# The pooling's per-head map and scale folded once into the output weight's last 256 rows

## The chip, the cores and the metric

The kernel runs on one core of a Trainium2 chip, in float32 from end to end. The metric is the device time of one execution in microseconds, the median of the runs; less is better. TensorE is called PE in the profile's rows (PEld is its weight load), VectorE is DVE, ScalarE is ACT, GpSimd is POOL and SyncE, which issues most DMAs, is SP.

## The reference, cut to what matters

One layer of a hybrid decoder trunk on 2048 tokens of width 1024. A normalised input is projected by one matrix into the columns of three head groups (windowed attention, retention, causal pooling), their outputs are concatenated and go through an output matrix, and a feed-forward block and a final normalisation follow. The change touches the pooling group alone:

```python
# u: (tokens, 256), four groups of 64 columns with windows 2, 4, 8, 16
groups.append(win_sum / cnt - uf[..., sl])
pooled = jnp.stack(groups, axis=2)
mixed = jnp.einsum('bsgc,gcd->bsgd', pooled, pool_w)        # a 64x64 map per group
mixed = mixed.reshape(B, S, POOL_WIDTH) * pool_scale        # a factor per column
...
y = jnp.concatenate([ya, yr, yp], axis=-1)                  # yp is `mixed`
return x + y @ w_out
```

The last 256 rows of `w_out` are multiplied by `mixed` and by nothing else, and nothing nonlinear lies between `pooled` and that product. So `(pooled @ W_g * scale) @ w_out_rows` equals `pooled @ (W_g @ diag(scale) @ w_out_rows)`.

## The kernel before, in words

Every large product is made of three products of rounded parts (high x low, low x high, high x high; lines 2145 to 2147 in the helper `three`), so every weight block and every activation exists as a `_hi` and a `_lo` tile. ACT makes the `_hi` (`split_hi`, line 958, for weights), DVE the `_lo` as source minus `_hi` (`split_lo`, line 1670).

The mixer runs over four quarters of 512 tokens (`q`); then come the feed-forward's up products and down products, more than half of the time. Each engine has one program, written out by hand in the order in which it is to run; engines meet by semaphores alone. `Events.now(q, i)` is the count after event `i` of quarter `q`.

Weights come in 27 units of 128x1024 per quarter. SP loads unit `u` into one of three `stage` slots (`load_weights`, line 559) once the split of unit `u-3` is over, ACT and DVE split it into a ring of six slots. Units 0 to 5 and 18 feed the products `proj_T` (outputs transposed: three q blocks, k, v, and the two pooling blocks), 6 to 17 feed `proj_G`, 19 to 26 are the rows of `w_out`: 25 and 26 are the pooling's.

In the first quarter everything starts at once: SP issues the inputs, tables, constants, the four 64x64 maps (`poolw`, line 577), the table of positional bias rows to DRAM and back (`store_rows` line 581, `load_bias` line 587, which waits for the store to have landed), and the units, all on one queue. Of the eight PSUM banks, three (`dense`) take the large products; S0, S1 hold scores, T0, T1 transposes, OB outputs.

The program of TensorE in a quarter begins with four `proj_T`, then `row_factors` (line 2166: the row factors spread over a bank), `proj_T(4)`, the first attention scores (`att_scores(q, 0)`, line 2242, into S0 and S1), `proj_T(5)`, the next scores. Retention and output products come last, and among them `pool_mix` (line 2346): one 128x512 float32 product per pooling half and quarter, block-diagonal `poolw` with the `pooled` tile, into T1. ACT then writes `T1 * pscale` as the high part (`yP_high`, line 1080), DVE the low part (`yP_low`, line 1606), into `hT_hi` and `hT_lo`, which the output products 8 to 15 read. `pooled` is the tile `vT`, used again for both halves and for v in the next quarter.

Of the kernel before, what the change touches and what calls it, by code (L numbers as in the profile page):

```python
# [7 lines left out]
P = 128  # L8
D = 1024
SEQ = 2048  # L10
HEAD = 64
NQH, NKV, NRET = 6, 2, 6
# [98 lines left out]
def build(nc, x, xt, wmix, wup, wdn, cst, tab, onehot, gmix, gmlp, gfin, sinks, rel_bias, pool_w, pool_scale, out):  # L111
    x2_dram = nc.dram_tensor("x2_dram", (SEQ, D), F32).ap()
    u_dram = nc.dram_tensor("u_dram", (NPASS, NK, NPAIR // GP, P, GP, HALF), F32).ap()
    rows_dram = nc.dram_tensor("bias_rows_dram", (NQH, P * 384), F32).ap()

    with ExitStack() as ctx:
# [47 lines left out]
        pt = work("pt", 76928, [P, 2, 2 * 3 * P])  # L164
        vT = work("vT", 83072, [P, QT])
# [90 lines left out]
        s_pm = sem("s_pm")  # L256

# [28 lines left out]
        comb_done = Events(sem("comb_done"), 8)  # L286
        max_done = Events(sem("max_done"), 8)
# [3 lines left out]
        den_done = Events(sem("den_done"), 8)  # L291
        rinv_done = Events(sem("rinv_done"), 8)
# [27 lines left out]
        ya_done = Events(sem("ya_done"), 4)  # L320
        y_done = Events(sem("y_done"), 4)
# [7 lines left out]
        mix_done = Events(sem("mix_done"), 2)  # L329
# [203 lines left out]
        def _(sp):  # L533
# [258 lines left out]
        def _(pool):  # L792
# [56 lines left out]
            def kz_of(q, b):  # L849

                pool.wait_ge(qk_done.sem, qk_done.now(q, b))
                pool.wait_ge(ru_done.sem, ru_done.before(q, b))
# [92 lines left out]
        def _(act):  # L945
# [53 lines left out]
            def evac_T(q, t):  # L999
# [4 lines left out]
                else:  # L1004
                    act.wait_ge(mix_done.sem, mix_done.before(q, 1))
# [173 lines left out]
            def mixer_act(q, last):  # L1179
# [7 lines left out]
                split_hi(q, 4)  # L1187
                evac_T(q, 2)
# [4 lines left out]
                split_hi(q, 8)  # L1193
                evac_T(q, 4)
# [231 lines left out]
        def _(dve):  # L1426
            for e in (wlo_done, carried, s_evac, xlo_done, x2_evac, sc_done, comb_done, max_done, pt_evac, nmax_done, sde_done, den_done, rinv_done, pn_done,
# [1238 lines left out]
```

## Time and profile before

| What | Value |
|---|---|
| Median of 3 runs | 2020.3 us (2020.28 to 2021.57) |
| Span of the profiled execution | 2018.4 us |
| Median less span (what lies around the span) | 1.9 us |
| TensorE busy | 2006.9 us, 99% |
| DVE / ACT / POOL busy | 70% / 44% / 9% |
| The chain that ended last | 98% TensorE |
| Granted TensorE clock | 0.999 mean |

The profile gives one execution. Its span goes from the first instruction to the last; the device time of the runs is a little longer. "Busy" of TensorE counts a matmul from start to its modelled end, and matmuls overlap, so the distance from one start to the next is what a matmul costs the engine, not its listed duration.

### The profile page before, as it was taken

How to read it: one execution, taken by the hardware profiler on the slowest of the kernel's cores; microseconds unless marked ns; L12 is line 12 of the kernel's file. 1: busy time of each engine (PE TensorE's matmuls, PEld its weight loads, DVE VectorE, ACT ScalarE, POOL GpSimd, SP SyncE). 2: the span in 40 equal slices, each digit the busy share in tenths (PEclk: the TensorE clock that was granted, in tenths of full speed). 3: DMA queues.
4: the chain of work that ended last, by engine and by line, in shares of the span. 5: the costliest groups of instructions: out<-in, count | busy, mean ns of one | idle time of the engine just before them, and what ended most of it. 6: DMA issues, size and time to landing. Idle time of an engine off the chain costs nothing.

```text
span 2018.4 us, 26877 instructions
## 1 busy us (share of the span) xinstructions
PE 2006.9 (99%) x9964; PEld 1691.7 (84%) x9964; DVE 1416.2 (70%) x2043; ACT 891.2 (44%) x1500; POOL 190.9 (9%) x279
## 2 busy tenths in 40 slices
PE   9999999999999999999999999999999999999998
PEld 8988898889889888888888888888888888888886
DVE  6685578558746977777778677677666668667667
ACT  5433543543354426545456544445333334433333
POOL 2042113203220330000000000000000000000001
PEclk9999999999999999999999999999999999999999
DMA  8133412522252233676856566787957578756572
GB/s 285 56 98 136 142 63 74 193 84 79 100 181 85 93 117 102 149 185 160 181 149 152 136 154 179 178 190 198 396 196 276 197 298 323 287 202 261 200 289 84
DMA packets 101950, 348.64 MB, mean 173 GB/s; under 512 B 10267, under 2 KB 12220, under 8 KB 84412
## 3 DMA queue, kind: packets, MB, share of 16 engines
q1 hardware_dynamic: 99372, 338.27, 52.6%
q10 hardware_dynamic: 2448, 8.65, 1.2%
q8 instruction: 80, 1.31, 0.3%
q14 instruction: 50, 0.41, 0.1%
HBM read 270.21 MB, written 76.68 MB: 172 GB/s over the span
## 4 chain that ended last, share of the span: by engine, by line
PE 98%; DVE 1%; ACT 1%; issue 0%; POOL 0%; POOLq 0%; ACTq 0%
PE bank L2145 30%; PE bank L2147 30%; PE bank L2146 30%; PE bank L2242 1%; PE bank L2270 1%; PE bank L2318 1%; PE bank L2299 1%; PE bank L2321 1%; PE bank L2285 1%; PE bank L2361 1%; PE bank L2326 1%; PE bank L2256 1%; DVE hT_lo L1443 1%; PE bank L2346 0%; PE bank L2135 0%; PE bank L2336 0%
## 5 line engine op out<-in xcount | busy, mean ns | idle before, releaser
L2145 PE MATMUL bank<-h_hi,w_lo 128*128 128x512 f32 x912 | 355.7, 390 | 0.2 <-DVE h_lo L1654 0.2
L2147 PE MATMUL bank<-h_hi,w_hi 128*128 128x512 f32 x912 | 354.9, 389 | 0.0
L2146 PE MATMUL bank<-h_lo,w_hi 128*128 128x512 f32 x912 | 354.9, 389 | 0.0
L2145 PE MATMUL bank<-d_hi,u_lo 128*128 128x512 f32 x896 | 348.5, 389 | 0.0
L2146 PE MATMUL bank<-d_lo,u_hi 128*128 128x512 f32 x896 | 348.5, 389 | 0.0
L2147 PE MATMUL bank<-d_hi,u_hi 128*128 128x512 f32 x896 | 348.5, 389 | 0.0
L1286 ACT ACTIVATE u_hi<-u_raw 128x1024 fp32r<-128x1024 f32 x112 | 118.5, 1058 | 327.7 <-PE bank L2147 315.2
L1906 DVE TENSOR_TENSOR u_lo<-u_raw,u_hi 128x1024 fp32r<-128x1024 f32 x112 | 137.1, 1224 | 179.6 <-ACT u_hi L1286 179.6
L2145 PE MATMUL bank<-ring_hi,hT_lo 128*128 128x384 f32 (+1 forms) x672 | 241.3, 359 | 0.0
L2147 PE MATMUL bank<-ring_hi,hT_hi 128*128 128x384 f32 (+1 forms) x672 | 234.1, 348 | 0.0
L2146 PE MATMUL bank<-ring_lo,hT_hi 128*128 128x384 f32 (+1 forms) x672 | 233.8, 348 | 0.0
L2145 PEld LDWEIGHTS bank<-h_hi,w_lo 128*128 128x128 f32 x912 | 171.2, 188 | 35.8 <-issue 0.4
L2147 PEld LDWEIGHTS bank<-h_hi,w_hi 128*128 128x128 f32 x912 | 171.2, 188 | 35.6
L2146 PEld LDWEIGHTS bank<-h_lo,w_hi 128*128 128x128 f32 x912 | 171.2, 188 | 35.0
L2145 PEld LDWEIGHTS bank<-d_hi,u_lo 128*128 128x128 f32 x896 | 168.2, 188 | 34.9
L2146 PEld LDWEIGHTS bank<-d_lo,u_hi 128*128 128x128 f32 x896 | 168.2, 188 | 34.9
L2147 PEld LDWEIGHTS bank<-d_hi,u_hi 128*128 128x128 f32 x896 | 168.2, 188 | 34.9
L1670 DVE TENSOR_TENSOR ring_lo<-stage,ring_hi 128x1024 fp32r<-128x1024 f32 x108 | 134.0, 1265 | 37.9 <-ACT ring_hi L958 37.4
L1663 DVE TENSOR_TENSOR w_lo<-wraw,w_hi 128x512 fp32r<-128x512 f32 x156 | 104.2, 687 | 76.7 <-ACT w_hi L1105 75.9
L1105 ACT ACTIVATE w_hi<-wraw 128x512 fp32r<-128x512 f32 x156 | 96.7, 626 | 91.7 <-PE bank L2147 87.4
L958 ACT ACTIVATE ring_hi<-stage 128x1024 fp32r<-128x1024 f32 x108 | 109.8, 1053 | 60.2 <-DMA stage<-in_wmix 44.2
L2145 PEld LDWEIGHTS bank<-ring_hi,hT_lo 128*128 128x128 f32 x672 | 126.2, 188 | 11.4 <-issue 2.4
(220 smaller groups left out, 3109.0 us busy)
## 6 DMA issues: line engine op xcount, KB each, us to landing
u_raw<-u_dram SPq DMA_DIRECT2D x56, 1024.0 KB, 4.8
d_raw<-in_wdn SPq DMA_DIRECT2D x56, 1024.0 KB, 6.9
stage<-in_wmix SPq DMA_DIRECT2D x108, 512.0 KB, 4.4
u_dram<-ur SPq DMA_DIRECT2D x32, 1280.0 KB, 9.7
wraw<-in_wup SPq DMA_DIRECT2D x128, 256.0 KB, 3.8
e_raw<-in_wdn SPq DMA_DIRECT2D x24, 1024.0 KB, 8.9
xq<-in_x SPq DMA_DIRECT2D x16, 512.0 KB, 3.6
x_dram<-xq ACTq DMA_DIRECT2D x16, 512.0 KB, 3.0
```

The costliest lines, as they stand in the source:

```text
L958: act.activation(ring_hi[:, SLOT[u % NU], :], stage[:, u % STAGE, :], ACT.Copy).then_inc(whi_done.sem, 1)
L1105: act.activation(w_hi[w_slot(n, k)][:, :, :].rearrange("p c n -> p (c n)"), w_source(n, k), ACT.Copy).then_inc(w_hi_done, 1)
L1286: act.activation(hi[:, cell, :], src[:, 2 * h:2 * h + 2, :], ACT.Copy).then_inc(m_hi_done, 1)
L1443: dve.scalar_tensor_tensor(out=hT_lo[:, c, :], in0=xT[:, c, :], scalar=gcol[:, c:c + 1], in1=hT_hi[:, c, :].bitcast(F32), op0=ALU.mult, op ...
L1663: dve.tensor_tensor(w_lo[s][:, :, :].rearrange("p c n -> p (c n)"), w_source(n, k), w_hi[s][:, :, :].rearrange("p c n -> p (c n)").bitcast ...
L1670: dve.tensor_tensor(ring_lo[:, s, :], stage[:, u % STAGE, :], ring_hi[:, s, :].bitcast(F32), ALU.subtract).then_inc(wlo_done.sem, 1)
L1906: dve.tensor_tensor(lo[:, cell, :], src[:, 2 * h:2 * h + 2, :], hi[:, cell, :].bitcast(F32), ALU.subtract).then_inc(m_lo_done, 1)
L2145: pe.matmul(dst, al, bh, start=(first and k == 0), stop=False, skip_group_check=chain)
L2146: pe.matmul(dst, ah, bl, start=False, stop=False, skip_group_check=chain)
L2147: last = pe.matmul(dst, ah, bh, start=False, stop=(final and k == n - 1), skip_group_check=chain)
L2242: last = pe.matmul((S0, S1)[g][:, P * h:P * h + P], qT[a:a + HEAD, h, b * P:(b + 1) * P], kT[a:a + HEAD, (b + e) * P:(b + e + 1) * P], sta ...
L2256: last = pe.transpose((T0, T1)[k][:, h * P:(h + 1) * P], score_buf(i // 2)[:, k, 256 * h:256 * h + P], ident[:, :])
```

## The change

The map and the scale are multiplied into the last two weight units once, at the beginning of the first quarter. SP loads both units (512 KB each) once more, raw, into a tile `wpool`; ACT multiplies each row by its scale; TensorE multiplies with the transposed maps (four 128x512 float32 products into OB, T0, S0 and S1); ACT copies the four results back into `wpool` and stores them to DRAM as `poolout_dram`. From there SP loads units 25 and 26 in every quarter. `pool_mix` is gone from TensorE's program, and `yP_high` and `yP_low` read `pooled` itself. `wpool` lies where `kz` and a part of `pt` lie, so their first writers wait for the store (`s_poolst`).

```diff
+    poolout_dram = nc.dram_tensor("poolout_dram", (2, P, D), F32).ap()
+        wpool = work("wpool", 70784, [P, 2, D])
             def load_weights(q, u):
                 sp.wait_ge(wlo_done.sem, wlo_done.now(q, u - STAGE))
-                sp.dma_start(stage[:, u % STAGE, :], wmix[u % NU]).then_inc(st_full[u % STAGE].sem, 16)
+                src = wmix[u % NU]
+                if NU - 2 <= u < NU:
+                    sp.wait_ge(s_poolst, 32)
+                    src = poolout_dram[u - (NU - 2)]
+                sp.dma_start(stage[:, u % STAGE, :], src).then_inc(st_full[u % STAGE].sem, 16)
...
-            sp.dma_start(pscale[:, :], pool_scale).then_inc(s_const, 16)
+            sp.dma_start(pscale[:, :], pool_scale).then_inc(s_pool, 16)
             load_weights(0, 4)
             sp.wait_ge(s_pm, 3)
             for g in range(4):
                 a = HEAD * (g % 2)
-                sp.dma_start(poolw[a:a + HEAD, g // 2, a:a + HEAD], pool_w[g]).then_inc(s_const, 16)
+                sp.dma_start(poolw[a:a + HEAD, g // 2, a:a + HEAD], pool_w[g]).then_inc(s_pool, 16)
+            for cc in range(2):
+                sp.dma_start(wpool[:, cc, :], wmix[NU - 2 + cc]).then_inc(s_pool, 16)
...
             def yP_high(q, cc):
-                act.wait_ge(mix_done.sem, mix_done.now(q, cc))
-                act.activation(hT_hi[:, 3 + cc, :], T1[:, :], ACT.Copy, scale=pscale[:, cc:cc + 1]).then_inc(yPhi_done.sem, 1)
+                act.wait_ge(pooled_done.sem, pooled_done.now(q, 2 * cc + 1))
+                act.wait_ge(pool16_done.sem, pool16_done.now(q, 4 * cc + 3))
+                act.wait_ge(tile_done.sem, tile_done.now(q, T_UP1))
+                act.activation(hT_hi[:, 3 + cc, :], pooled[:, :], ACT.Copy).then_inc(yPhi_done.sem, 1)
+
+            def pool_weights_scaled():
+                act.wait_ge(s_pool, 16 * 7)
+                for cc in range(2):
+                    act.activation(wpool[:, cc, :], wpool[:, cc, :], ACT.Copy, scale=pscale[:, cc:cc + 1]).then_inc(s_poolscaled, 1)
+
+            def pool_weights_out():
+                for i in range(4):
+                    cc, half = divmod(i, 2)
+                    act.wait_ge(s_poolmm, i + 1)
+                    act.activation(wpool[:, cc, 512 * half:512 * half + 512], (OB, T0, S0, S1)[i][:, :], ACT.Copy).then_inc(s_poolout, 1)
+                    if half:
+                        act.wait_ge(s_poolout, i + 1)
+                        act.dma_start(poolout_dram[cc], wpool[:, cc, :]).then_inc(s_poolst, 16)
...
                 split_hi(q, 4)
+                if q == 0:
+                    pool_weights_scaled()
                 evac_T(q, 2)
...
                 split_hi(q, 8)
+                if q == 0:
+                    pool_weights_out()
                 evac_T(q, 4)
...
             def yP_low(q, cc):
                 dve.wait_ge(yPhi_done.sem, yPhi_done.now(q, cc))
-                dve.scalar_tensor_tensor(out=hT_lo[:, 3 + cc, :], in0=T1[:, :], scalar=pscale[:, cc:cc + 1],
-                                         in1=hT_hi[:, 3 + cc, :].bitcast(F32), op0=ALU.mult, op1=ALU.subtract).then_inc(yPlo_done.sem, 1)
+                dve.tensor_tensor(hT_lo[:, 3 + cc, :], pooled[:, :], hT_hi[:, 3 + cc, :].bitcast(F32), ALU.subtract).then_inc(yPlo_done.sem, 1)
...
             def att_scores(q, j):
                 if j == 0:
...
                     pe.wait_ge(s_brow, NQH)
+                    pe.wait_ge(s_poolout, 4)
...
-            def pool_mix(q, cc):
...
-                pe.matmul(T1[:, :], poolw[:, cc, :], pooled[:, :], start=True, stop=True).then_inc(mix_done.sem, 1)
+            def pool_weights():
+                pe.wait_ge(s_poolscaled, 2)
+                pe.wait_ge(s_brow, NQH)
+                for i in range(4):
+                    cc, half = divmod(i, 2)
+                    pe.matmul((OB, T0, S0, S1)[i][:, :], poolw[:, cc, :], wpool[:, cc, 512 * half:512 * half + 512],
+                              start=True, stop=True).then_inc(s_poolmm, 1)
...
                 row_factors(q)
+                if q == 0:
+                    pool_weights()
                 proj_T(q, 4)
...
-        "pool_w": a(pool_w)[0], "pool_scale": a(pool_scale).reshape(2, P).T,
+        "pool_w": a(pool_w)[0].transpose(0, 2, 1), "pool_scale": a(pool_scale).reshape(2, P).T,
```

Left out of the diff: waits on `mix_done` become waits on `yPlo_done`, or fall away; `row_factors` and `qk_transposes` no longer wait for `yPlo_done`; seven semaphores of the softmax and of the gate are merged into three with the same instructions; and DVE's `nsink` waits for the five constant loads, no longer for the maps.

TensorE's program in the first quarter, from the last product of `proj_T(3)` on (line 2166 is the row factors, `dg` their diagonal blocks), before:

```order
L2147 MATMUL bank<-hT_hi,ring_hi 128x512
L2166 MATMUL bank<-dg,ones 128x128 [waits s_init,s_brow,diag_done,yPlo_done,qkT_evac]
L2166 MATMUL bank<-dg,ones 128x128 x3
L2145 MATMUL bank<-hT_hi,ring_lo 128x512 [waits z_evac,wlo_done]
...
L2147 MATMUL bank<-hT_hi,ring_hi 128x512
L2242 MATMUL bank<-kT,qT 128x128 [waits R_done,s_brow,pm_done,s_evac,z_evac]
L2242 MATMUL bank<-kT,qT 128x128 x5
```

and after (the lines 2193, 2173 to 2175 and 2270 are the former 2166, 2145 to 2147 and 2242):

```order
L2175 MATMUL bank<-hT_hi,ring_hi 128x512
L2193 MATMUL bank<-dg,ones 128x128 [waits s_init,diag_done,s_brow,qkT_evac]
L2193 MATMUL bank<-dg,ones 128x128 x3
L2372 MATMUL bank<-wpool,poolw 128x512 [waits s_brow,s_poolscaled]
L2372 MATMUL bank<-wpool,poolw 128x512 x3
L2173 MATMUL bank<-hT_hi,ring_lo 128x512 [waits z_evac,wlo_done]
...
L2175 MATMUL bank<-hT_hi,ring_hi 128x512
L2270 MATMUL bank<-kT,qT 128x128 [waits s_poolout,R_done,s_brow,pm_done,s_evac,z_evac]
L2270 MATMUL bank<-kT,qT 128x128 x5
```

Four products stand between the row factors and `proj_T(4)`, and the first scores wait for ACT's four copies (`s_poolout`) as well.

ACT's program at the same time, from the split of unit 4 on, before:

```order
L958 ACTIVATE ring_hi<-stage 128x1024 [waits tile_done,st_full1]
L1007 ACTIVATE qT<-bank 128x512 [waits tile_done]
L958 ACTIVATE ring_hi<-stage 128x1024 [waits tile_done,st_full2]
L997 ACTIVATE rb<-bank 128x512 [waits s_evac,rbmm_done]
L958 ACTIVATE ring_hi<-stage 128x1024 [waits wlo_done,tile_done,st_full0]
L958 ACTIVATE ring_hi<-stage 128x1024 [waits wlo_done,tile_done,st_full1]
L958 ACTIVATE ring_hi<-stage 128x1024 [waits wlo_done,tile_done,st_full2]
L1007 ACTIVATE vT<-bank 128x512 [waits mix_done,tile_done]
```

and after:

```order
L968 ACTIVATE ring_hi<-stage 128x1024 [waits tile_done,st_full1]
L1098 ACTIVATE wpool<-wpool,pscale 128x1024 [waits s_pool]
L1098 ACTIVATE wpool<-wpool,pscale 128x1024
L1017 ACTIVATE qT<-bank 128x512 [waits tile_done]
L968 ACTIVATE ring_hi<-stage 128x1024 [waits tile_done,st_full2]
L1007 ACTIVATE rb<-bank 128x512 [waits s_evac,rbmm_done]
L968 ACTIVATE ring_hi<-stage 128x1024 [waits wlo_done,tile_done,st_full0]
L968 ACTIVATE ring_hi<-stage 128x1024 [waits wlo_done,tile_done,st_full1]
L968 ACTIVATE ring_hi<-stage 128x1024 [waits wlo_done,tile_done,st_full2]
L1105 ACTIVATE wpool<-bank 128x512 [waits s_poolmm] x2
L1108 DMA poolout_dram<-wpool 128x1024 [waits s_poolout]
L1105 ACTIVATE wpool<-bank 128x512 [waits s_poolmm] x2
```

The copies that free the score banks stand behind the splits of units 5 to 8, each of which waits for its load.

SP's queue behind the four maps, after (before, the row with `wpool` is missing and all else is the same):

```order
L584 DMA poolw<-in_pool_w 64x64 [waits s_pm]
L584 DMA poolw<-in_pool_w 64x64 x3
L586 DMA wpool<-in_wmix 128x1024 x2
L602 DMA tabs<-in_tab 128x544 [waits pool16_done,qk_done]
L590 DMA bias_rows_dram<-zt 128x6x384 [waits s_brow]
L566 DMA stage<-in_wmix 128x1024 [waits wlo_done]
L596 DMA bias<-bias_rows_dram 128x256 [waits s_rowst]
```

The two raw units are queued ahead of the bias rows' store, unit 5, the bias loads and units 6 to 8.

## Rows read from the trace of the kernel before

**Rows 1.** The profile's first part: busy us (share of span) and instructions per engine.

```profile
PE 2006.9 (99%) x9964; PEld 1691.7 (84%) x9964; DVE 1416.2 (70%) x2043; ACT 891.2 (44%) x1500; POOL 190.9 (9%) x279
```

**Rows 2.** Waits of TensorE, whole span: waiter <- releaser: us in total, times, longest.

```profile
PE bank L2135 <- POOL ones L797: 2.6, 1, 2.6
PE bank L2361 <- ACT hraw L1091: 0.3, 1, 0.3
PE bank L2145 <- DVE h_lo L1654: 0.2, 1, 0.2
```

**Rows 3.** TensorE's groups by line and shape, the pooling product (two instructions per product).

```profile
L2346 PE MATMUL bank<-vT,poolw 128*128 128x512 f32 x16 | 8.2, 592 | 0.0
```

**Rows 4.** Timeline of TensorE around the pooling products: start us, us, instruction, count.

```profile
143.43 0.83 PE L2326 MATMUL bank<-zt,kz 128*128 128x128 f32 x6
...
145.66 0.39 PE L2145 MATMUL bank<-ring_hi,yA_lo 128*128 128x512 f32 x1
...
152.61 1.02 PE L2346 MATMUL bank<-vT,poolw 128*128 128x512 f32 x2
153.46 0.55 PE L2318 MATMUL bank<-zt,sc 128*128 128x64 f32 x4
...
155.47 0.83 PE L2326 MATMUL bank<-zt,kz 128*128 128x128 f32 x6
...
156.84 0.39 PE L2145 MATMUL bank<-ring_hi,yA_lo 128*128 128x512 f32 x1
```

**Rows 5.** Timeline of TensorE, row factors and first scores.

```profile
33.17 1.05 PE L2166 MATMUL bank<-dg,ones 128*128 128x128 f32 x8
33.97 0.48 PE L2145 MATMUL bank<-hT_hi,ring_lo 128*128 128x512 f32 x1
...
39.60 0.94 PE L2242 MATMUL bank<-kT,qT 64*128 64x128 f32 x12
```

**Rows 6.** Timeline of ACT, the splits of units 5 to 8, with idle time before.

```profile
31.37 1.06 ACT L958 ACTIVATE ring_hi<-stage 128x1024 fp32r<-128x1024 f32 x1 [2.85 <-DMA stage<-in_wmix]
34.26 0.60 ACT L997 ACTIVATE rb<-bank 128x512 f32<-128x512 f32 x1 [1.82 <-PE bank L2166]
37.42 1.06 ACT L958 ACTIVATE ring_hi<-stage 128x1024 fp32r<-128x1024 f32 x1 [2.57 <-DMA stage<-in_wmix]
39.26 1.06 ACT L958 ACTIVATE ring_hi<-stage 128x1024 fp32r<-128x1024 f32 x1 [0.78 <-DMA stage<-in_wmix]
40.47 1.06 ACT L958 ACTIVATE ring_hi<-stage 128x1024 fp32r<-128x1024 f32 x1 [0.16 <-DMA stage<-in_wmix]
```

**Rows 7.** Timeline of DVE: wait for the maps, unit 5, first attention copy.

```profile
27.26 0.17 DVE L1827 TENSOR_SCALAR nsink<-sinkb 128x6 f32<-128x6 f32 x1 [5.13 <-DMA poolw<-in_pool_w]
...
32.46 1.23 DVE L1670 TENSOR_TENSOR ring_lo<-stage,ring_hi 128x1024 fp32r<-128x1024 f32 x1 [3.39 <-ACT ring_hi L958]
...
57.45 1.02 DVE L1507 TENSOR_TENSOR pt<-bank,window 128x384 f32<-128x384 f32 x2 [1.60 <-PE bank L2256]
```

**Rows 8.** Timeline of SP's DMA queue: start us, time to issue, count.

```profile
30.14 2.71 SPq L587 DMA_DIRECT2D bias<-bias_rows_dram  x6
32.89 1.38 SPq L559 DMA_DIRECT2D stage<-in_wmix  x3
```

**Rows 9.** Windows: length, busy per engine, PEclk, share of the DMA engines, GB/s.

```profile
25.00:27.50 2.50, 2.50 (x13) 2.06 (x11) 0.18 (x2) 1.06 (x1) 0.43 (x2) 1.00 1.06 398
27.50:30.00 2.50, 2.50 (x13) 2.07 (x12) 1.57 (x4) 0.60 (x2) 0.00 (x0) 1.00 0.80 316
```

**Rows 10.** Timeline of ACT around a DMA that it issues itself (ACTq).

```profile
180.18 0.34 ACTq L979 DMA_DIRECT2D x_dram<-xq  x1
180.65 1.06 ACT L958 ACTIVATE ring_hi<-stage 128x1024 fp32r<-128x1024 f32 x1 [0.50 <-ACT junk L976]
```

**Rows 11.** Timeline of TensorE at the start: the warm-up products and what follows.

```profile
2.63 6.45 PE L2135 MATMUL bank<-ones 128*128 128x128 f32 x32 [2.63 <-POOL ones L797]
9.00 0.44 PE L2138 MATMUL bank<-oneh_r,relw_lo 33*128 33x384 f32 x1
```

More of the change, by code:

```diff
@@ L256, in build @@
         s_pm = sem("s_pm")
+        s_pool = sem("s_pool")
+        s_poolscaled = sem("s_poolscaled")
+        s_poolmm = sem("s_poolmm")
+        s_poolout = sem("s_poolout")
+        s_poolst = sem("s_poolst")
         xq_full = [Events(sem(f"xq_full{b}"), 1, 16) for b in range(NB)]
@@ L1004, in evac_T @@
                 else:
-                    act.wait_ge(mix_done.sem, mix_done.before(q, 1))
+                    act.wait_ge(yPlo_done.sem, yPlo_done.before(q, 1))
                     dst = vT[:, :]
@@ L1492, in softmax @@
                 dve.wait_ge(exp_done.sem, exp_done.now(q, 4 * i + 3))
-                dve.tensor_tensor(rsum[:, k, :], rsum[:, k, :], ses[:, k, :], ALU.add).then_inc(den_done.sem, 1)
-                dve.wait_ge(den_done.sem, den_done.now(q, i))
-                dve.reciprocal(rinv[:, k, :], rsum[:, k, :]).then_inc(rinv_done.sem, 1)
-                dve.wait_ge(rinv_done.sem, rinv_done.now(q, i))
+                dve.tensor_tensor(rsum[:, k, :], rsum[:, k, :], ses[:, k, :], ALU.add).then_inc(norm_done.sem, 1)
+                dve.wait_ge(norm_done.sem, norm_done.now(q, 2 * i))
+                dve.reciprocal(rinv[:, k, :], rsum[:, k, :]).then_inc(norm_done.sem, 1)
+                dve.wait_ge(norm_done.sem, norm_done.now(q, 2 * i + 1))
                 for h in range(3):
@@ L1505, in evac_pt @@
                     dve.wait_ge(o_done.sem, o_done.now(q, i // 2 - 1))
+                else:
+                    dve.wait_ge(s_poolst, 32)
                 for half in range(2):
@@ L1574, in pool_first @@
                     dve.wait_ge(tab_full.sem, tab_full.now(q, 0))
-                    dve.wait_ge(mix_done.sem, mix_done.before(q, 1))
                     dve.wait_ge(vtr_done.sem, vtr_done.now(q, 0))
                 else:
-                    dve.wait_ge(mix_done.sem, mix_done.now(q, 0))
+                    dve.wait_ge(yPlo_done.sem, yPlo_done.now(q, 0))
                 for k in range(2):
@@ L1590, in pool_rest @@
             def pool_rest(q, cc):
-                if cc == 0:
-                    dve.wait_ge(mix_done.sem, mix_done.before(q, 1))
-                else:
-                    dve.wait_ge(mix_done.sem, mix_done.now(q, 0))
                 for k in range(2):
@@ L2160, in row_factors @@
                 pe.wait_ge(qkT_evac.sem, qkT_evac.before(q, 7))
-                pe.wait_ge(yPlo_done.sem, yPlo_done.before(q, 1))
                 pe.wait_ge(s_brow, NQH)
@@ L2281, in qk_transposes @@
                     pe.wait_ge(yRlo_done.sem, yRlo_done.now(q, b - 2))
-                    pe.wait_ge(yPlo_done.sem, yPlo_done.now(q, 1))
                 for k in range(2):
@@ L2330, in y_transposes @@
             def y_transposes(q, b):
-                pe.wait_ge(y_done.sem, y_done.now(q, b))
+                pe.wait_ge(gated_done.sem, gated_done.now(q, 2 * b + 1))
                 pe.wait_ge(qkT_evac.sem, qkT_evac.now(q, 2 * min(b + 1, 3) + 1))
@@ L2337, in y_transposes @@
                 last.then_inc(ytr_done.sem, 1)
-            def pool_mix(q, cc):
-                pe.wait_ge(pooled_done.sem, pooled_done.now(q, 2 * cc + 1))
-                pe.wait_ge(pool16_done.sem, pool16_done.now(q, 4 * cc + 3))
-                if cc == 0:
-                    pe.wait_ge(qkT_evac.sem, qkT_evac.now(q, 3))
-                else:
-                    pe.wait_ge(yPlo_done.sem, yPlo_done.now(q, 0))
-                pe.matmul(T1[:, :], poolw[:, cc, :], pooled[:, :], start=True, stop=True).then_inc(mix_done.sem, 1)
+            def pool_weights():
[5 more added lines that the diff above has]
+                              start=True, stop=True).then_inc(s_poolmm, 1)
             def h_transposes(p, i):
```

35 lines of the change are left out of this document (15 added, 20 removed).

## The prediction

> **What bounds the kernel now.** I read the busy shares first, then TensorE's waits, then the start-to-start distances on TensorE. TensorE is busy 99% of the span [rows 1] and waits 3.3 us in all, 2.6 of them before its first instruction [rows 2]. "Busy" alone proves little for a pipelined engine, so the waits are the better evidence: once started, TensorE has 0.7 us of waits in 2018.4 us (the row of 0.3 and two of 0.2, of which one stands). Two things follow. An instruction taken from TensorE's program gives back its full start-to-start distance; work taken from ACT, DVE or POOL, or made quicker there, gives nothing. And any new wait of TensorE is paid in full, since it has no slack in which to catch up. The only question is how many microseconds of TensorE's order go, how many come, and whether it has to wait somewhere it did not.
>
> **What goes: eight pooling products.** There are 16 instructions, two per float32 product, so 8 products, with no idle time before them [rows 3]. Their listed 592 ns overlap. At the second place of a quarter the next work starts 153.46 - 152.61 = 0.85 us after the product [rows 4]. At the first place, from the state product (line 2326) to the second group of the following output tile it is 145.66 - 143.43 = 2.23 us with a pooling product between, and 156.84 - 155.47 = 1.37 us at the same pair of steps without one [rows 4]: 0.86 us. So 8 x 0.855 = **6.8 us go**.
>
> **What comes on TensorE: four products.** The new ones have the same shape, 128x128 by 128x512 in float32, so 4 x 0.855 = **3.4 us come**. They stand between the row factors and the projection of unit 4. If nothing waits the change is worth -3.4 us.
>
> **Does TensorE wait in front of them?** They need the two units scaled by ACT, and ACT needs the two raw loads. TensorE reaches the place at 33.97 [rows 5]. The maps, queued just ahead of the raw units, have landed at 27.26, where DVE stopped waiting for them [rows 7]. Two units are 2 x 128 x 1024 x 4 B = 1.05 MB; the DMA engines are saturated there and move 398 GB/s [rows 9], so 2.6 us: landed at about 29.9. Two scalings of 128x1024 take what a split takes, 1.06 us each [rows 6], or a little more for the factor per row: over at about 32.1. That is 1.9 us ahead of TensorE, so no wait here. Should the loads be up to 1.9 us late it is still nothing, and a wait here would come off the next one anyway, as long as that is set by ACT's splits.
>
> **The wait that I expect: the first scores.** TensorE would reach them at 39.60 [rows 5] + 3.4 = 43.0. They now wait for ACT's four copies, and those are behind the splits of units 5 to 8, which wait for DMA. Four steps:
> 1. The 1.05 MB are ahead of the bias rows' store, unit 5, the bias loads and units 6 to 8 on one queue that is full until about 30 us (share 1.06, then 0.80) [rows 9]. So the store, on whose landing the bias loads wait, lands 2.6 us later: 30.14 becomes 32.8. SP stands still in that wait, so units 6 to 8 are issued from 35.5 instead of 32.89 [rows 8].
> 2. Each of ACT's splits of units 5 to 8 ended a wait for its load (2.85, 2.57, 0.78 and 0.16 us) [rows 6], so each moves with it: 31.37 to 34.0, 37.42 to 40.0, 39.26 to 41.9, 40.47 to 43.1. The load of unit 8 also waits for DVE's part of unit 5 (32.46 + 1.23 [rows 7]), which moves by the same 2.6. The last split ends at 44.1.
> 3. Four copies from PSUM at 0.60 us each [rows 6], about 0.1 of it overlapped. Between the second and the third ACT waits for its own copy and issues a store; a like store left ACT idle for 0.50 us [rows 10]. So 44.1 + 1.1 + 0.5 + 1.1 = 46.8.
> 4. TensorE starts the scores at 46.8 instead of 43.0: **3.8 us of waiting**.
>
> Nothing behind the scores adds to it. ACT's copy of v and DVE's additions of bias hang on this same point and move with TensorE; the splits of units 9 and 10 and their loads have then more time than before.
>
> **Edits at nothing.** The high part of the pooled values is taken from `pooled` in place of T1, on ACT, and waits no more for TensorE; ACT and DVE are busy 44% and 70% [rows 1], TensorE does not wait for either, and the instructions stay about as long. If that cover were gone, 8 such pairs at 0.1 us or so would be under 1 us. The waits taken from TensorE (for `yPlo_done`) were never the last to come [rows 2]. The merged semaphores change no instruction. The first attention copy into `pt` and POOL's first `kz` wait for the stores of `wpool`: those are issued by 47, while the first `pt` write, at 57.45 before [rows 7], is behind the scores and moves with them to some 64. Loads of units 25 and 26 have the same size from another place.
>
> **The sum.** -6.8 + 3.4 + 3.8 = +0.4 us. The profiled span of 2018.4 becomes 2018.8. The median of the runs is 1.9 us above the span, so 2020.3 + 0.4 = **2020.7 us**. It is a difference of three terms of which only the wait is uncertain. From below: if the raw loads pushed nothing back, the split of unit 8 would end at 41.5 [rows 6], the copies at 44.2, and TensorE would wait 1.2 us: sum -2.2, 2018.1. From above: 1.05 MB at the 316 GB/s of the later window [rows 9] takes 3.3 us, and with another microsecond or two lost in waits for landings the wait is 6: sum +2.6, 2022.9. I take 2.6 us of push because in the nearest row the DMA engines have no gap and the queue serves in order.
>
> **A rule on the clock, and what it would make of this wait.** TensorE starts slowly here: the first 32 instructions of 128x128 take 9.00 - 2.63 = 6.4 us, 0.20 each [rows 11], while eight of the same shape at 33 us start 0.10 us apart [rows 5]. That is the half level, 1.2 GHz for 2.4, after 2.6 us without work [rows 2], though the PEclk column says 1.00; nowhere later does TensorE pause, so no row shows what a pause of 3.8 us does.
> The Trainium skill, in "TensorE: Matmul & The Clock Gate", section "Part 1: The HAM clock gate", says that the array's clock falls to half when the engine has been without work, and comes back only after sustained work. The start agrees with the second half of this; the first half speaks against the change.
>
> **The rivals.**
> A. *The loads are hidden anyway* (the push does not reach unit 8). For it: the DMA engines are only 80% busy in 27.5 to 30 us [rows 9]. Against it: SP's wait for the store's landing passes the delay on. 2018.1 us.
> B. *No wait at all* (ACT's copies done by 43.0). It would need the splits 4 us earlier than they were; sum -3.4, 2016.9 us. Nearly excluded.
> C. *The clock drops in the new wait.* Place: the first scores of the first quarter. Price: a slow stretch as long as at the start, 6.4 us, does the work of 3.2, so 3.2 us are lost. With the wait at 3.8 it gives 2023.9; with the wait at 5 or more, where a drop is also likelier, -3.4 + 5 + 3.2 = +4.8, 2025.1 us, and slower. It decides from where wait and lost clock together pass 7.4 us. For it: the start's slow stretch [rows 11]. [...]
> D. *A longer wait without the clock*: another load or landing in the chain slips; 2022.9 us.
> E. *Something in the quarters is freed that the waits do not show*, more than 4 us in all. TensorE's 0.7 us of waits leave no room for it; 2016 or less.
> That the products are not removed is no rival: the order of instructions shows them gone.
>
> **How the numbers follow.** Forecast 0.54, A 0.17, B 0.03, C 0.13, D 0.09, E 0.04. About 0.2% (4 us) is what a measurement of this kernel can tell from no change. Faster by more than that, under 2016.3, needs E: 0.04. Slower, over 2024.3, needs C with a wait of 5, or D at its far end: about 0.07 + 0.03, and 0.02 for what I have not seen: 0.12. The rest, 0.84, is within. The range for 8 in 10 takes in A with a bit of B below and C with the forecast's wait above: 2017.4 to 2024.6.
>
> **What the profile of the changed kernel would show.** Right: no products in the quarters' output part and each quarter after the first 1.7 us shorter on TensorE; four new products from about 34.0 to 37.4 without a wait ahead; a wait of TensorE of 3 to 5 us at the first scores, ended by ACT's copy of the last `wpool` part; the splits of units 5 to 8 some 2.6 us later. Wrong: a first wait in front of the new products; splits at their old times (A); matmuls at twice their distance behind the wait (C); new waits in the later quarters, or for the stores. The prediction fails above all if the push on the loads is not near 2.6 us, since nothing else in the sum can move by much.

## The result and the profile after

| | kernel before | changed kernel |
|---|---|---|
| median, us | 2020.63 (10 runs, 2019.99 to 2021.99) | 2025.41 (10 runs, 2022.07 to 2026.61) |
| ratio, 95% interval | | 1.0021 [1.0013, 1.0029] |
| profiled span, us | 2018.4 | 2024.0 |
| mean granted clock | 0.999 | 0.997 |

The change made the kernel slower by 4.8 us in the median, 5.6 us between the two profiled spans. I had forecast 2020.7 us, no change, in a range up to 2024.6: the time lies above it. Rival C happened.

The waits of TensorE in the changed kernel (waiter <- releaser: us in total, times, longest), to be held against [rows 2]:

```profile
PE bank L2270 <- ACT wpool L1105: 5.5, 1, 5.5
...
PE bank L2363 <- DVE zt L1596: 0.6, 4, 0.2
```

The first row is the new wait, at the place forecast and ended by the releaser forecast, but 5.5 us and not 3.8. The second was not forecast. (A third new one, 0.3 us for a `ring_lo` at 16.6 us, has cost nothing by the row factors, which begin 0.10 us earlier than before.) Next, TensorE's timeline (start us, us, instruction, count, idle before it), against [rows 5]:

```profile
33.07 1.05 PE L2193 MATMUL bank<-dg,ones 128*128 128x128 f32 x8
33.96 3.60 PE L2372 MATMUL bank<-wpool,poolw 128*128 128x512 f32 x8
...
42.62 0.39 PE L2175 MATMUL bank<-hT_hi,ring_hi 128*128 128x512 f32 x1
48.53 1.65 PE L2270 MATMUL bank<-kT,qT 64*128 64x128 f32 x12 [5.52 <-ACT wpool L1105]
...
51.56 0.63 PE L2173 MATMUL bank<-hT_hi,ring_lo 128*128 128x512 f32 x1
...
57.69 0.94 PE L2270 MATMUL bank<-kT,qT 64*128 64x128 f32 x12
```

Three things are to be seen. The four new products begin at 33.96 without a wait. The last product of the projection behind them starts at 42.62 and not at 39.28, so the scores would have come at about 42.95 for 39.60, 3.35 us later (3.44 us counted from the row factors). They come 5.5 us after that. And they run slowly: twelve products take 1.65 us where the same twelve take 0.94 at 57.69, and the projection's products behind them 0.63 for 0.39. From the first scores to the second it is 57.69 - 48.53 = 9.16 us; in the kernel before it was 6.54, as this row shows for its second scores, beside the first at 39.60 [rows 5]:

```profile
46.14 0.94 PE L2242 MATMUL bank<-kT,qT 64*128 64x128 f32 x12
```

So 2.6 us are lost behind the wait. The windows of the changed kernel say why (length, busy per engine, PEclk, share of the DMA engines, GB/s):

```profile
45.00:47.50 2.50, 0.00 (x0) 0.00 (x0) 1.93 (x2) 2.08 (x4) 0.00 (x0) 0.97 0.70 215
47.50:50.00 2.50, 1.47 (x12) 1.39 (x12) 0.00 (x0) 2.04 (x4) 0.00 (x0) 0.50 0.89 208
50.00:55.00 5.00, 5.00 (x15) 3.88 (x14) 2.83 (x4) 1.23 (x2) 0.00 (x0) 0.58 0.90 345
55.00:60.00 5.00, 5.00 (x35) 4.11 (x34) 2.21 (x3) 1.06 (x1) 0.00 (x0) 1.00 0.20 78
```

The granted clock is at full (2.4 GHz) until shortly before 47.5 us and then at 0.50 (1.2 GHz); TensorE had done nothing since 43 us. It is full again before 55 us. Half of the 1.47 us busy in the second window and 42% of the 5 us in the third are 2.8 us of lost clock, near the 2.6 between the scores. The clock fell inside the pause, about a microsecond before the scores began.

Why the wait is 5.5: the chain from the loads to the copies. SP's DMA queue (start us, time to issue, count), against [rows 8]:

```profile
33.94 2.70 SPq L596 DMA_DIRECT2D bias<-bias_rows_dram  x6
```

The bias rows' store is waited for until 33.94 and not 30.14: 3.8 us later, where I had written 2.6 (SyncE stands in that wait; the issue of the bias loads begins when it ends). ACT's timeline, against [rows 6]:

```profile
35.16 1.06 ACT L968 ACTIVATE ring_hi<-stage 128x1024 fp32r<-128x1024 f32 x1 [2.09 <-DMA stage<-in_wmix]
...
42.07 1.06 ACT L968 ACTIVATE ring_hi<-stage 128x1024 fp32r<-128x1024 f32 x1 [5.37 <-DMA stage<-in_wmix]
43.39 1.06 ACT L968 ACTIVATE ring_hi<-stage 128x1024 fp32r<-128x1024 f32 x1 [0.26 <-DMA stage<-in_wmix]
44.63 1.06 ACT L968 ACTIVATE ring_hi<-stage 128x1024 fp32r<-128x1024 f32 x1 [0.18 <-DMA stage<-in_wmix]
45.60 1.07 ACT L1105 ACTIVATE wpool<-bank 128x512 f32<-128x512 f32 x2
...
47.09 1.09 ACT L1105 ACTIVATE wpool<-bank 128x512 f32<-128x512 f32 x2 [0.42 <-ACT wpool L1105]
```

The splits of units 5 to 8 come 3.8, 4.7, 4.1 and 4.2 us later than before. ACT stands idle for 5.37 us in front of the split of unit 6, with the products' results ready in the banks since about 37: in that idle time the four copies (2.6 us from 45.60 to 48.18) would have fitted. The scores start 0.35 us after the last copy ends.

Last, the quarters. TensorE's timeline at the same step of the first and the second quarter, of the kernel before and then of the changed one:

```profile
133.44 1.51 PE L2270 MATMUL bank<-pt,vtok 128*64 128x384 f32 x8
...
321.99 1.51 PE L2270 MATMUL bank<-pt,vtok 128*64 128x384 f32 x8
```

```profile
144.99 1.51 PE L2298 MATMUL bank<-pt,vtok 128*64 128x384 f32 x8
...
332.08 1.51 PE L2298 MATMUL bank<-pt,vtok 128*64 128x384 f32 x8
```

The first quarter, taken from this step to the same step of the next, is 187.09 us long for 188.55: 1.46 less, not the 1.7 of two products (the next two quarters are 1.52 and 1.55 shorter). What is missing is behind `zt` of line 1596. In the kernel before, TensorE (first row, at its line 2336) came 0.61 us after DVE had written it (second row, 149.04 + 0.55):

```profile
150.20 0.49 PE L2336 MATMUL bank<-ident,zt 128*128 128x128 f32 x3
```

```profile
149.04 0.55 DVE L1562 TENSOR_TENSOR zt<-zt,s 128x384 f32<-128x384 f32 x1
```

The product taken out ahead of it was worth 0.85, more than these 0.61, so TensorE now stands: from the step shown above to this one it took 16.76 us (133.44 to 150.20) and now takes 16.16, which is 0.60 less and no more. In the changed kernel, TensorE and then DVE:

```profile
161.15 0.55 PE L2363 MATMUL bank<-ident,zt 128*128 128x128 f32 x3 [0.15 <-DVE zt L1596]
```

```profile
157.58 0.68 DVE L1635 TENSOR_TENSOR hT_lo<-vT,hT_hi 128x512 fp32r<-128x512 f32 x1
...
160.53 0.56 DVE L1596 TENSOR_TENSOR zt<-zt,s 128x384 f32<-128x384 f32 x1 [0.15 <-POOL s L881]
```

The account of the profiled spans: +3.35 (products), +5.6 (wait), +2.6 (clock), which is +11.55 at the step of 144.99 against 133.44, and from there to the end 5.95 us less (1879.01 for 1884.96): together +5.6, as measured.

### The profile page after: what moved, and what is told of

Read it like the earlier page. It is cut to its first block, busy times and chain, and to the rows that moved or that the text cites. A ratio compares the mean times of both kernels' runs of the same rounds, so it can differ in the third digit from the quotient of the medians.

```text
span 2024.0 us, 26868 instructions
## 1 busy us (share of the span) xinstructions
PE 2006.2 (99%) x9956; PEld 1691.0 (84%) x9956; DVE 1416.0 (70%) x2043; ACT 894.8 (44%) x1506; POOL 194.8 (10%) x279
## 4 chain that ended last, share of the span: by engine, by line
PE 87%; DVE 6%; DMA 2%; POOL 2%; issue 1%; ACT 1%; SPq 0%; POOLq 0%; ACTq 0%; DVEq 0%
PE bank L2173 27%; PE bank L2174 27%; PE bank L2175 27%; DMA stage<-in_wmix 2%; PE bank L2270 1%; DVE ring_lo L1698 1%; POOL qT L898 1%; PE bank L2345 1%; DVE zt L1555 1%; DVE sc_odd L1531 1%; DVE pt L1541 1%; PE bank L2298 1%; PE bank L2388 1%; DVE zt L1585 1%; DVE hT_lo L1475 1%
```

## The experiments

Each ratio is to the kernel before, run on the same chip between the experiments; its medians were 2020.76, 2020.87 and 2020.91 us in the three sets. My theory after the result: **the push of the loads makes the wait, and the wait makes the clock fall**. Rivals: the push alone costs this time whatever TensorE waits for (1); the slow products behind the wait are slow for another reason than the wait (2).

**The copies ahead of the splits.** ACT's four copies stand in its program where its idle time is.

```diff
                 rb_copy(q)
+                if q == 0:
+                    pool_weights_out()
                 split_hi(q, 6)
                 split_hi(q, 7)
                 split_hi(q, 8)
-                if q == 0:
-                    pool_weights_out()
```

> ACT's four copies stand right behind the copy of the row factors, ahead of the splits of units 6 to 8; the raw loads and their push on the other loads stay. Theory (the loss is TensorE's wait at the first scores plus the half clock that follows it): ACT has nothing to do from 36.7 to 42.1 us, so the copies are over by about 39.5, before TensorE arrives at 42.9; no wait, no half clock, and the bias loads and units 6 to 8, though 4 us late, are not waited for. 5.5 + 2.7 us come back: -6.0 (quarters) + 3.4 (products) = -2.7 us against before, ratio 0.9987. Rival 1 (the late loads themselves are what TensorE pays for): a wait of some 4 us shows up behind the first scores instead, ratio 1.001 or more. Rival 2 (the half clock has to do with the new products, not with the pause): the wait goes, a slow stretch stays, ratio about 1.000.

Measured: 2018.69 us (11 runs, 2017.83 to 2024.34), ratio 0.9992 [0.9983, 1.0000], span 2016.9. ACT copies from 37.02 to 39.61, and TensorE's scores (first and second) have no wait and 0.28 us of it:

```profile
43.63 0.94 PE L2270 MATMUL bank<-kT,qT 64*128 64x128 f32 x12
50.51 0.94 PE L2270 MATMUL bank<-kT,qT 64*128 64x128 f32 x12 [0.28 <-DVE sc L1505]
```

The two are 6.88 us apart and each takes 0.94: the clock stays. Units 6 to 8 are as late here as in the changed kernel or later (41.88, 43.64, 46.48 for 42.07, 43.39, 44.63). One run in eleven took 2024.34 at a mean clock of 0.997; it wasn't profiled. So the place of the copies in ACT's program is worth 6.7 us between the medians, and rival 1 has little left to explain.

**TensorE kept at work through the wait.** 25 products of ones into a bank that is free there.

```diff
                 proj_T(q, 4)
+                if q == 0:
+                    pe.wait_ge(rb_done.sem, rb_done.now(q, 0))
+                    for _ in range(25):
+                        pe.matmul(T1[:, 0:P], ones[:, :], ones[:, :], start=True, stop=True)
                 att_scores(q, 0)
```

> The changed kernel with 25 products of ones between the projection of unit 4 and the first scores (into T1, results unused): they fill 5.1 us of the 5.5 us pause with work. The first scores start at the same time as without them. Theory (the pause itself costs 5.5, and the half clock 2.7 us on top): clock at 1.00 all through, 2.7 us less than the changed kernel: about +2.9 us against before, ratio 1.0014. Rival (the half clock is not the pause's doing): slow stretch as before and no gain, ratio 1.0025.

Measured: 2024.71 us (2023.68 to 2025.41), 1.0018 [1.0009, 1.0027], span 2022.1. TensorE's timeline:

```profile
43.05 5.74 PE L2402 MATMUL bank<-ones 128*128 128x128 f32 x50
48.72 0.94 PE L2270 MATMUL bank<-kT,qT 64*128 64x128 f32 x12
...
55.25 0.94 PE L2270 MATMUL bank<-kT,qT 64*128 64x128 f32 x12
```

and the windows at the same place:

```profile
45.00:47.50 2.50, 2.50 (x24) 2.50 (x24) 1.79 (x2) 2.08 (x5) 0.00 (x0) 1.00 0.75 210
...
50.00:55.00 5.00, 5.00 (x24) 4.06 (x22) 2.54 (x4) 1.11 (x2) 0.00 (x0) 1.00 0.98 360
```

The scores start as late as in the changed kernel (48.72 for 48.53), yet the second ones come 6.53 us later and not 9.16. The work between is the same and the DMA engines are as full; only TensorE's idle time is gone. That fells rival 2: the idle time drops the clock, at a price of 2.6 us in this pair of profiles. In the medians the filler gains only 0.7 us of it, and the interval covers the ratios of the theory and of the rival alike: the rows decide, not the time. Some 0.3 is that the filler ran past the copies (over at 48.05 in its ACT timeline; the scores follow 0.67 us later, 0.35 in the changed kernel). Some more is that the price of the clock is not always 2.6 (the changed kernel again, below); the rest stays open.

**The loads made small.** 64 of 1024 columns of each raw unit are loaded, the rest is zeroed by POOL; the output leaves out most of what the folded rows give.

```diff
-                sp.dma_start(wpool[:, cc, :], wmix[NU - 2 + cc]).then_inc(s_pool, 16)
+                sp.wait_ge(s_pm, 9)
+                sp.dma_start(wpool[:, cc, 0:64], wmix[NU - 2 + cc][:, 0:64]).then_inc(s_pool, 16)
```

> The raw loads cut to their first 64 columns, 64 KB in place of 1 MB; the rest of wpool is zero, so the folded rows are left out but for these columns. Everything else stays, ACT's copies too. Theory (the raw loads push the bias rows' store and units 5 to 8 back by 4 us, and by this the last split before the copies): store landed at about 30, split of unit 8 over at 41.6, copies at 44.2 to 44.5, TensorE waits 1.3 us and the clock stays: -6.0 + 3.4 + 1.3 = -1.3 us, ratio 0.9993. Rival (the delay comes from ACT's own new work in front of the splits): the wait stays over 4 us and the half clock too, ratio 1.002.

Measured: 2019.92 us (2018.86 to 2021.47), 0.9996 [0.9987, 1.0005], span 2017.1. SP's queue, and TensorE at the first scores:

```profile
30.53 2.70 SPq L597 DMA_DIRECT2D bias<-bias_rows_dram  x6
```

```profile
44.32 0.94 PE L2272 MATMUL bank<-kT,qT 64*128 64x128 f32 x12 [0.42 <-ACT wpool L1107]
```

Without the bytes the store lands as before (30.53 for 30.14), the splits stand at 37.87, 39.16 and 40.42 as in [rows 6], and the copies are over at 43.96, 4.2 us earlier than in the changed kernel. The wait is 0.4 us; it would be about 1.3, as expected, had TensorE not begun its row factors 0.9 us late in this profile (33.96 for 33.07), for reasons of the start. So of the wait of 5.5 us the push makes 4.2, and 1.3 stand without it.

**The loads alone, in the kernel before.** The two raw units are loaded at the same place of the queue into `wpool`, from which nobody reads. Besides, GpSimd and VectorE wait for these loads before they first write the memory under it; no wait of TensorE hangs on that.

```diff
+            for cc in range(2):
+                sp.dma_start(wpool[:, cc, :], wmix[NU - 2 + cc]).then_inc(s_pool, 16)
```

> The kernel before with the two raw loads alone, issued where the change issues them, into wpool, which nobody reads. Theory (a push on the loads costs nothing by itself, for TensorE has slack to them): store landed near 34, splits of units 6 to 8 at 42 to 44.6 as in the changed kernel; TensorE goes on with the first scores at 39.6 and is waited for by nobody; no wait over 0.5 us, ratio 1.000. Rival (units 6 to 8 or the bias come too late for the first grouped projection or the softmax): TensorE waits 1 to 4 us near 47 us, ratio 1.0005 to 1.002.

Measured: 2023.26 us (2020.91 to 2024.37), 1.0011 [1.0002, 1.0020], span 2020.2. SP's queue, TensorE at the second scores, and DVE ahead of them:

```profile
33.03 2.70 SPq L591 DMA_DIRECT2D bias<-bias_rows_dram  x6
```

```profile
48.03 0.94 PE L2249 MATMUL bank<-kT,qT 64*128 64x128 f32 x12 [0.95 <-DVE sc L1478]
```

```profile
42.57 3.76 DVE L1677 TENSOR_TENSOR ring_lo<-stage,ring_hi 128x1024 fp32r<-128x1024 f32 x3 [5.39 <-ACT ring_hi L963]
46.24 0.55 DVE L1471 COPY bias<-bias 128x768 f32<-128x768 f32 x1
46.83 1.14 DVE L1478 SCALAR_TENSOR_TENSOR sc<-bank,rstd,bias 128x384 f32<-128x384 f32 x2
```

The store lands 2.9 us late. The span is 1.8 us longer: 0.95 is this wait, and 0.9 is there already ahead of the first scores (40.47 for 39.60), and as early as the row factors. I can't ascribe that to the loads: the row factors begin between 32.89 and 34.04 in the profiles of this document, at 33.06 and 34.03 in two kernels whose programs differ only behind them (the last two experiments). The median is 2.5 us higher. Five of the eleven runs had a mean clock of 0.998 and took 2023.5 to 2024.4 us; none of these was profiled, so lost clock behind a pause of 1 us isn't excluded. My expectation missed, its rival came. The wait has its cause in the push: DVE's low parts of units 6 to 8 come late, and its bias work is behind them. So rival 1 is partly right: the push costs something with no copy behind it. I had written that nothing behind the scores adds to the wait; with the products in front, the same place shows 0.28 (copies ahead of the splits, above) and 0.82 (the same with the order of DVE changed, below).

**Copies behind the split of unit 6, and of unit 7.** They cut the wait in steps.

```diff
                 split_hi(q, 6)
+                if q == 0:
+                    pool_weights_out()
                 split_hi(q, 7)
                 split_hi(q, 8)
-                if q == 0:
-                    pool_weights_out()
```

> The changed kernel with ACT's copies behind the split of unit 6 in place of unit 8. Theory of the pause and the clock: split of unit 6 over at 43.1, copies at 45.7, TensorE pauses 2.8 us (5.5 in the changed kernel); a pause of 2.6 us in front of the first instruction is followed by a slow stretch, but there TensorE had never worked, so both are possible: with full clock -6.0 + 3.4 + 2.8 = +0.2 us, ratio 1.0001; with the half clock in most runs +2.9 us, ratio 1.0014.

Measured: 2019.95 us (10 runs), 0.9996 [0.9987, 1.0005]; at the scores:

```profile
44.57 0.94 PE L2270 MATMUL bank<-kT,qT 64*128 64x128 f32 x12 [1.74 <-ACT wpool L1105]
```

The pause was shorter than the 2.8 us expected, since unit 6 was split at 40.67 here and not at 42.07. Behind it the clock stays at 1.00 in all windows. Eight runs took 2019.0 to 2020.5 at a mean clock of 0.999, two took 2022.05 and 2022.06 at 0.998.

```diff
                 split_hi(q, 7)
+                if q == 0:
+                    pool_weights_out()
                 split_hi(q, 8)
-                if q == 0:
-                    pool_weights_out()
```

> The same with the copies behind the split of unit 7: pause of about 4.1 us. If a drop of the clock needs a pause near the 5.5 us of the changed kernel, full clock and +1.5 us, ratio 1.0007; if 4 us are enough, the half clock for 5 us or so behind it in most runs, +4.2 us, ratio 1.002, and runs spread over 3 us as they do in the changed kernel (one whose clock stays up, others not).

Measured: 2023.14 us (10 runs), 1.0008 [0.9999, 1.0017]; the profiled run (2025.52) has a pause of 4.88 us and the half clock:

```profile
48.11 1.65 PE L2270 MATMUL bank<-kT,qT 64*128 64x128 f32 x12 [4.88 <-ACT wpool L1105]
```

The pause was hardly shorter than the changed kernel's (unit 7 was split only at 44.22), so the step failed as a step. From the first scores to the second it is 9.44 us, a price of 2.9. But the runs divide by the mean clock: 2020.5 and 2020.7 at 0.999, the other eight from 2022.4 to 2025.5 at 0.997 or 0.998.

**A shorter filler.** 15 products of ones in place of 25 (`range(15)`).

> As e2 with 15 products of ones in place of 25: they take 3.4 us and stop well before ACT's copies are over, so nothing is added to the way, and a pause of about 2.2 us is left. Theory (the half clock comes of the long pause and costs 2.7 us on top of it): first scores start when they do in the changed kernel, clock at full, 2.7 us less than the changed kernel beside it in most runs, and less spread. Rival (the time behind the pause is lost to something else, DVE's bias or the loads): no gain over the changed kernel.

Measured: 2024.81 us (2022.85 to 2026.42), 1.0018 [1.0009, 1.0027]; my expectation failed. TensorE's timeline and the windows:

```profile
42.93 3.51 PE L2402 MATMUL bank<-ones 128*128 128x128 f32 x30
48.84 0.94 PE L2270 MATMUL bank<-kT,qT 64*128 64x128 f32 x12 [2.40 <-ACT wpool L1105]
...
56.98 0.94 PE L2270 MATMUL bank<-kT,qT 64*128 64x128 f32 x12
```

```profile
48.00:50.00 2.00, 1.17 (x13) 1.07 (x14) 0.19 (x1) 1.54 (x3) 0.00 (x0) 1.00 0.98 342
50.00:52.00 2.00, 2.00 (x6) 1.53 (x5) 1.96 (x4) 0.44 (x1) 0.00 (x0) 0.50 1.06 381
52.00:54.00 2.00, 2.00 (x7) 1.55 (x7) 0.68 (x1) 1.06 (x1) 0.00 (x0) 0.65 0.74 250
```

A pause of 2.4 us was enough here, and the clock fell behind it, when TensorE was at work again: the scores still ran at full speed. From them to the second ones it is 8.14 us, a price of 1.6. Five runs took 2025.9 to 2026.4 at 0.998, six took 2022.9 to 2024.8 at 0.999, which is 2.6 us between the groups' medians (2026.1 and 2023.5). That this is the price of the clock in the changed kernel's profile is no proof: the one profile here, of the slower group, shows 1.6 of it between the scores.

**The changed kernel again**, beside these.

> The changed kernel once more, unaltered, on the chip of its neighbours, for the size and the spread of its runs: 4.5 to 5 us over before, spread over 3 to 4 us.

Measured: 2025.11 us (11 runs, 2023.35 to 2025.64), 1.0020 [1.0011, 1.0028]; in its profile the wait at the scores is 5.11 us, and the clock is at half behind it. SP's queue, ACT's split of unit 6, and TensorE's first and second scores:

```profile
32.89 2.70 SPq L596 DMA_DIRECT2D bias<-bias_rows_dram  x6
```

```profile
41.74 1.06 ACT L968 ACTIVATE ring_hi<-stage 128x1024 fp32r<-128x1024 f32 x1 [6.08 <-DMA stage<-in_wmix]
```

```profile
48.15 1.65 PE L2270 MATMUL bank<-kT,qT 64*128 64x128 f32 x12 [5.11 <-ACT wpool L1105]
...
56.62 0.94 PE L2270 MATMUL bank<-kT,qT 64*128 64x128 f32 x12
```

This profile shows two things. The store landed only 2.75 us later than in the kernel before, near the 2.6 of the prediction, and yet units 6 to 8 were split 4.3, 3.7 and 3.8 us later (41.74, 42.99, 44.25) and the wait was 5.1. And the scores are 8.47 us apart, so the clock cost 1.9 us here and not 2.6. It had fallen earlier in the pause, which began at 43.0 as in the first profile (where the window of 45 to 47.5 us has 0.97), and was back earlier:

```profile
45.00:46.00 1.00, 0.00 (x0) 0.00 (x0) 0.96 (x2) 1.00 (x3) 0.00 (x0) 0.76 0.94 111
```

**The order of DVE in a quarter.** On top of the copies ahead of the splits, the low part of the pooled values goes behind `zt`.

```diff
                 ret_sums(q, 0)
-                yP_low(q, 0)
                 ret_ya(q, 0)
...
                 ret_y(q, 0)
+                yP_low(q, 0)
```

> As e1 (ACT's copies ahead of the splits), and DVE's low part of the first pooling half moved behind the last gate product of block 0. In the changed kernel and in e1 TensorE stands 0.3 us per quarter at the first transposes of the gated retention, because it gets there 0.86 us earlier than before while DVE does not. Theory: the 0.3 us per quarter go, 1.2 us in all: ratio to e1 0.9994, to before 0.9986. Rival (the pause is not DVE's order, but GpSimd's factor, which DVE waits for): no change against e1.

Measured: 2017.40 us (2016.39 to 2018.46), 0.9981 [0.9972, 0.9990]. The waits for `zt` are gone, and the median is 1.3 us under that of the copies ahead of the splits. In the profiles the first three quarters are 0.33 to 0.41 us shorter (186.74, 186.65 and 186.74 for 187.07, 187.06 and 187.07).

**Everything late.** The raw loads are issued behind unit 8, the scaling is behind the split of unit 11, the products stand in two pairs in the attention part, the copies behind ACT's gate copies; with `wpool` in two tiles and the order of DVE just told.

```diff
-            for cc in range(2):
-                sp.dma_start(wpool[:, cc, :], wmix[NU - 2 + cc]).then_inc(s_pool, 16)
...
+                    if q == 0 and u == 8:
+                        for cc in range(2):
+                            sp.dma_start(wpool[cc][:, :], wmix[NU - 2 + cc]).then_inc(s_pool, 16)
...
                 split_hi(q, 11)
+                if q == 0:
+                    pool_weights_scaled()
...
                     att_transposes(q, i)
+                    if q == 0 and i == 0:
+                        pool_weights(0)
```

> The whole fold moved out of the crowded start: the raw units are loaded behind unit 8, scaled behind the split of unit 11, multiplied in two pairs of products into OB and T1 between the grouped projections (57 to 65 us), copied there; DVE's order as in e5. Theory (what the change costs beyond its products is only where it stands): no wait of TensorE over 0.3 us, loads of units 5 to 8 and the bias at the times of before, spread of the runs as before: -6.8 + 3.4 = -3.4 us, ratio 0.9983. Rival (the fold takes its price wherever it stands, through ACT's queue or the loads of units 9 to 11): a new wait of 1 to 3 us between 47 and 75 us, ratio 0.999 or more.

Measured: 2016.57 us (2016.18 to 2018.22), 0.9979 [0.9970, 0.9988], span 2014.8: faster than both kernels. The first pair in TensorE's timeline; the second is at 63.05, and neither is behind a wait:

```profile
57.14 1.88 PE L2376 MATMUL bank<-wpool,poolw 128*128 128x512 f32 x4
```

and SP's queue, where the store is on time and the raw loads are behind the units that someone waits for:

```profile
30.53 2.70 SPq L594 DMA_DIRECT2D bias<-bias_rows_dram  x6
...
34.69 1.12 SPq L610 DMA_DIRECT2D wpool<-in_wmix  x2
```

**The same without the move on DVE** (`yP_low` back ahead of `ret_ya`).

> As e6 (fold moved out of the start) with DVE's low part of the first pooling half back where it was, ahead of the gate product. Theory (DVE's order costs 0.3 us per quarter once the pooling products are gone): four waits of TensorE of 0.3 us at the first transposes of the gated retention, 1.2 us over e6, ratio to before 0.9985. Rival: as e6, 0.9979.

Measured: 2018.23 us (2017.84 to 2019.16), 0.9987 [0.9978, 0.9996]. Its waits for `zt` are back:

```profile
PE bank L2365 <- DVE zt L1598: 1.0, 4, 0.3
```

1.7 us lie between the two medians. The first three quarters are 187.25, 187.12 and 187.07 us long for 186.74, 186.89 and 186.75. So the order of DVE costs the change 0.2 to 0.5 us per quarter, 0.35 in the mean. (The profiled spans differ by 2.4 us, but 1.0 of that is the late start of the row factors told above.)

## Why the prediction was wrong

**The products** were right. The four new ones cost 3.35 us at the scores, 3.44 counted from the row factors (forecast 3.4), without a wait ahead of them; the eight are gone.

**"The wait that I expect", step 1, is the step that failed.** It took the push as bytes by mean bandwidth: 1.05 MB at 398 GB/s, 2.6 us, and called it the same for everything behind. The store landed 3.8 us later and units 6 to 8 came 4.1 to 4.7 us later. Without the bytes the push is gone (the small loads: copies over 4.2 us earlier), so it is theirs; its size was off, and so was "the same for everything behind". The changed kernel run again shows these two apart: there the store was late by 2.75 us, as forecast, and units 6 to 8 by 3.7 to 4.3 all the same. In the kernel before with the loads alone it is 2.9, and 3.5 to 4.1. So another 0.9 to 1.6 us was lost between the store's landing and unit 6, which no step of the prediction has; what took it, no run here tells. My bound from above, 3.3 us "and another microsecond or two", was the better description. The steps behind it held: ACT split each unit as it landed, and the copies took 2.6 us with the store between (2.7 written). The last split ended at 45.69 for 44.1; 0.35 us from the last copy to the scores I had at nothing. The wait was 5.5 for 3.8.

**The clock, rival C**, followed from the same step. I gave it 0.13, "with the wait at 5 or more, where a drop is also likelier", price 3.2 us, sum 2025.1. The wait was 5.5 and the price 2.6. I took the price from the time that the start spends at half clock; the 2.6 us are what the rows between the scores show, with the filler and without, and other profiles have 2.9, 1.9 and 1.6. By the Trainium skill ("TensorE: Matmul & The Clock Gate", section "Part 1: The HAM clock gate") idleness takes the clock to half. The traces agree: 0.50 is granted at the end of the pauses of 5.5, 5.1 and 4.9 us and behind that of 2.4 us; the pause of 1.7 us shows none. The chance of C was too small, for one because I set the chance of a wait of 5 too low, and then because a pause of 2.4 us could do it, so one of 3.8 might have too. That C's 2025.1 us lies so near the measured 2025.4 is partly luck: its wait was 0.5 too short, its price 0.6 too high, and 0.9 us of the quarters were not in it.

**"Edits at nothing" missed 0.15 to 0.25 us per quarter**, about 0.9 us in all. I said of each removed product that it gives back its whole distance, since nobody waits. But the wait of zero at `zt` had a slack of 0.61 us, less than the 0.85 taken away. The rows were there to read, in DVE's timeline. The move on DVE (2018.23 to 2016.57) shows that DVE's order makes this wait.

**"Nothing behind the scores adds to it"** was right for the changed kernel, but only because the first scores waited: when they no longer do, the second wait 0.28 us in one profile and 0.82 in another.

The sum with the measured terms: -6.8 + 0.9 (quarters) + 3.35 + 5.55 + 2.6 = +5.6 us, for +0.4. The wait gives 1.75 of the miss, the clock 2.6, the quarters 0.9.

**Not settled.** Which pause drops the clock: 1.7 us did not in the profiled run (two slower runs of that kernel, at 0.998, were not profiled), 2.4 did, and one run of ten of the changed kernel (span 2020.3, clock 0.999) kept it nearly whole. No run here tells what decides it, nor where in a pause the clock falls. It is also open what held units 6 to 8 back beyond the store, and why the long filler gains 0.7 us in the medians where its profile shows 2.6 between the scores; the spread of the price explains a part at most.

## What to carry to other kernels

Of a new wait on an engine that never stops, price the wait and what the engine's clock does behind it as one term: here a wait taken 1.75 us too short cost 4.35. Put one-off work where the engines that serve it are idle anyway, and its loads behind the loads that someone waits for: the same change cost 4.8 us with its loads and copies at one place and gained 2.7 with them at another. Before an instruction is counted as given back whole, look for how much earlier the next operand is ready than it is used; that slack is the most that can be given back.

## What the runs showed of the hardware

- A pause of TensorE of 2.4 us, after 3.5 us of products of ones, was followed by 3 to 4 us at half clock which began only after the engine was at work again. In the profile with a pause of 1.7 us the clock stayed at 1.00.
- The half clock costs less than twice the time: 6.54 us of work between the scores took 9.16, since the clock came back on the way (0.58 in the mean of 50 to 55 us). In a second profile of the same kernel, with the same beginning of the pause, the clock fell earlier (0.76 in 45 to 46 us) and the same work took 8.47.
- 1.05 MB ahead on a full queue moved a waited-for landing by 2.75 us in one profile, by 2.9 in another and by 3.8 in a third, where the mean rate gives 2.6; the loads behind it moved by 3.5 to 4.7.
- A DMA that ACT issues itself left ACT idle for 0.42 us between two copies, beside 0.50 in [rows 10].
